# LayerNorm in front of the MLPs: the gain applied with the offset on the turned rows, and to x itself later

## The reference, cut to what matters

```
def layer_norm(x, g, b):
    mu = mean(x); var = mean((x - mu) ** 2)            # over the 2048 channels of a row
    return (x - mu) * rsqrt(var + LN_EPS) * g + b

for i in range(2):
    mix = ssd_mixer(x, ...) if i == 0 else pool_mixer(x, ...)
    x = layer_norm(ALPHA * x + mix, ln_mix_g[i], ln_mix_b[i])                       # the norm in front of the MLP
    x = layer_norm(ALPHA * x + square(relu(x @ w1[i])) @ w2[i], ln_ffn_g[i], ln_ffn_b[i])
```

## Time and profile before

| | |
|---|---|
| median of 3 runs | 2191.07 us (2189.57 to 2195.26) |
| the profiled execution | 2191.99 us, of which its span is 2190.1 us |
| PE busy | 2159.6 us, 99% of the span |
| DVE busy | 1428.4 us, 65% |
| ACT busy | 1119.0 us, 51% |
| POOL busy | 223.3 us, 10% |
| granted PE clock, mean | 0.997 of full speed |

### The profile page before, as it was taken

The page is one execution under the profiler, slowest core; times in us unless marked ns, Lnnn a source line. Parts: engine busy times, 40 slices in busy tenths (PEclk is TensorE's granted clock), DMA queues, the critical chain, the costliest instruction groups (busy, mean ns, idle before and its releaser), DMA issues.

```text
span 2190.1 us, 30795 instructions
## 1 busy us (share of the span) xinstructions
PE 2159.6 (99%) x10626; PEld 1816.4 (83%) x10626; DVE 1428.4 (65%) x1730; ACT 1119.0 (51%) x1565; POOL 223.3 (10%) x172
## 2 busy tenths in 40 slices
PE   9999999999999999999999999989999999999997
PEld 7788888888888788888888888878888888888886
DVE  7787787687777656557565655686565655555656
ACT  5677576675775634444343443456444443443433
POOL 0213233132220100002000000032000000000001
PEclk9999999999999999999999999999999999999999
DMA  7968988589586574545555645445555645555553
GB/s 274 254 202 236 252 230 244 179 235 277 174 249 209 195 252 170 199 172 196 187 193 190 211 172 196 169 154 207 197 197 186 216 167 198 185 190 193 192 192 115
DMA packets 246963, 443.99 MB, mean 203 GB/s; under 512 B 14049, under 2 KB 49041, under 8 KB 245217
## 3 DMA queue, kind: packets, MB, share of 16 engines
q1 hardware_dynamic: 206608, 397.52, 53.5%
q0 software_dynamic: 35664, 28.66, 7.6%
q10 hardware_dynamic: 4608, 16.78, 2.0%
HBM read 440.68 MB, written 2.23 MB: 202 GB/s over the span
## 4 chain that ended last, share of the span: by engine, by line
PE 90%; DVE 4%; ACT 2%; issue 2%; DMA 2%; ACTq 0%; DVEq 0%; SPq 0%
PE acc L375 14%; PE acc L377 14%; PE acc L376 14%; PE acc L638 9%; PE acc L645 5%; PE tb L638 5%; PE sbk L638 5%; PE sbk L377 3%; PE tb L375 3%; PE tb L376 3%; PE sbk L375 3%; PE sbk L376 3%; PE tb L377 3%; PE sbk L645 2%; PE tb L645 2%; DVE wlo L1145 2%
## 5 line engine op out<-in xcount | busy, mean ns | idle before, releaser
L748 ACT CAST whi<-raw 128x1024 fp32r<-128x1024 f32 x746 | 773.8, 1053 | 666.7 <-DMA raw<-in_w 292.3
L1145 DVE TENSOR_TENSOR wlo<-raw,whi 128x1024 fp32r<-128x1024 f32 x746 | 917.0, 1266 | 205.3 <-ACT whi L748 201.5
L375 PE MATMUL acc<-whi,xT 128*128 128x512 f32 x832 | 334.5, 402 | 14.9 <-DVE wlo L1145 9.9
L377 PE MATMUL acc<-wlo,xT 128*128 128x512 f32 x832 | 325.2, 391 | 0.0
L376 PE MATMUL acc<-whi,xT 128*128 128x512 f32 x832 | 324.8, 390 | 0.0
L375 PE MATMUL acc<-whi,hTl 128*128 128x512 f32 x736 | 291.4, 396 | 0.3 <-DVE hTl L1165 0.3
L376 PE MATMUL acc<-whi,hTh 128*128 128x512 f32 x736 | 286.6, 389 | 0.0
L377 PE MATMUL acc<-wlo,hTh 128*128 128x512 f32 x736 | 286.5, 389 | 0.0
L638 PE MATMUL acc<-xT,whi 128*128 128x512 f32 x896 | 224.0, 392 | 0.0
L375 PEld LDWEIGHTS acc<-whi,xT 128*128 128x128 f32 x832 | 156.7, 188 | 53.5 <-issue 10.8
L638 PEld LDWEIGHTS acc<-xT,whi 128*128 128x128 f32 x896 | 162.0, 189 | 29.6
(11 more groups left out here) (210 smaller groups left out, 2667.1 us busy)
## 6 DMA issues: line engine op xcount, KB each, us to landing
raw<-in_w SPq DMA_DIRECT2D x512, 512.0 KB, 4.7
raw<-in_in_proj SPq DMA_DIRECT2D x162, 512.0 KB, 5.6
raw<-in_out_proj SPq DMA_DIRECT2D x64, 512.0 KB, 7.1
spare<-in_masks ACTq DMA_DIRECT2D x16, 512.0 KB, 7.7
spare<-f_scratch POOLq DMA_DIRECT2D x32, 256.0 KB, 15.4
area_d<-in_masks ACTq DMA_DIRECT2D x8, 512.0 KB, 6.3
area_d<-f_scratch POOLq DMA_DIRECT2D x16, 256.0 KB, 7.5
area_c<-in_masks ACTq DMA_DIRECT2D x8, 512.0 KB, 7.0
```

The costliest lines, as they stand in the source:

```text
L375: pe.matmul(dst, lhs[1][:, kt, rows(t)], hi, start=first and i == 0, stop=False)
L377: mm = pe.matmul(dst, lhs[0][:, kt, rows(t)], lo, start=False, stop=end)
L748: act.copy(whi[:, s.slot(RING)], raw[:, r]).then_inc(hi_ready, 1)
L1145: dve.tensor_tensor(wlo[:, slot], raw[:, r], whi[:, slot].bitcast(F32), ALU.subtract).then_inc(lo_ready, 1)
```

## The change

The gain is applied by ACT together with the offset: the four L783 instructions of a quarter get `scale=lng[...]` (one number per partition) beside `bias=lnb[...]`. The turned rows are therefore made from x without its gain, and PE's `x_ready` waits for ACT's norm (`ln_act`) instead of the gain. The seven `gains` instructions and the one `gain_q3` of each norm go; eight `late_gain` instructions on DVE, in the first chunk between the splits s + 12 to s + 19, multiply x itself. POOL's additions of the offset wait for these (`x_gain`). A small load of the gains by rows, `lng`, joins the loads at the start, and the waits for these count one more. The norms behind the MLPs are as before but for the numbers of their semaphores.

```
-LN_BASE = [[0, 10, 20, 30], [0, 11, 21, 32]]
+LN_BASE = [[0, 7, 17, 24], [0, 7, 17, 24]]
...
             def x_ready(i):
                 def ready(t, j):
-                    if t == 0 and j == 3:
-                        pe.wait_ge(t0_gain_q3, i + 1)
-                    else:
-                        pe.wait_ge(ln_vec[t], LN_BASE[t][i] + 8 + j)
+                    pe.wait_ge(ln_act[t], 4 * i + j + 1)
...
                         off = act.activation(offset_x[u % 2][:, k * P:(k + 1) * P], tb[u % 2][:, k * P:(k + 1) * P],
-                                             ACT.Identity, bias=lnb[:, first // 16, kt:kt + 1])
+                                             ACT.Identity, bias=lnb[:, first // 16, kt:kt + 1],
+                                             scale=lng[:, first // 16, kt:kt + 1])
...
-            dve.wait_ge(const_in, 16 * 7)
+            dve.wait_ge(const_in, 16 * 8)
...
+            def late_gain(i, t, j):
+                cs = slice(j * NB, (j + 1) * NB)
+                dve.wait_ge(gb_in, 32 * (i + 1))
+                dve.wait_ge(ln_act[t], 4 * i + j + 1)
+                dve.tensor_tensor(x[:, t, cs], x[:, t, cs], gb[:, 0, cs], ALU.mult).then_inc(x_gain, 1)
...
                 mean_var(i, 0)
                 factors(i, 0)
-                early = len(adds) > 2
-                if early:
-                    adds[0](1)
-                gains(i, 0, (0, 1))
-                if early:
-                    adds[1](1)
-                gains(i, 0, (2,))
-                for add in adds[2 if early else 0:-1]:
+                for add in adds[:-1]:
                     add(1)
...
                 split_lo(s + 5)
-                gains(i, 1, (0, 1))
                 split_lo(s + 6)
                 split_lo(s + 7)
-                gains(i, 1, (2, 3))
                 for j in range(4):
                     lo_x(first, 1, j)
...
-                blocks(s + 8, 2, 4, lambda k: lo_h(u, k) if k < 2 else None)
+                def second(k):
+                    if k < 2:
+                        lo_h(u, k)
+                    for t in range(TT):
+                        late_gain(i, t, k)
+                blocks(s + 8, 2, 4, second)
...
             pool.dma_start(lnb[:], a["ln_b_rows"]).then_inc(const_in, 16)
+            pool.dma_start(lng[:], a["ln_g_rows"]).then_inc(const_in, 16)
...
             def offsets(i, first, s):
-                gain_q3(i)
                 pool.wait_ge(tr_lo, first + 8)
                 for j in range(4):
                     if j > 0:
                         pool.wait_ge(w_used, s + 6 + 4 * j)
                     for t in range(TT):
                         cs = slice(j * NB, (j + 1) * NB)
+                        pool.wait_ge(x_gain, 4 * i + 2 * j + t + 1)
                         pool.tensor_tensor(x[:, t, cs], x[:, t, cs], gb[:, 1, cs], ALU.add).then_inc(x_norm[t], 1)
```

More of the change, by code:

```diff
@@ L136, in build @@
         lnb = sb("lnb", [P, 2, KT])
+        lng = sb("lng", [P, 2, KT])
         warm = sb("warm", [P, 1])
@@ L215, in build @@
         gb_in = sem("gb_in")
+        x_gain = sem("x_gain")
         stored = sem("stored")
@@ L704, in pool_x @@
                 else:
-                    pe.wait_ge(t0_gain_q3, 2)
+                    pe.wait_ge(t0_gain_q3, 1)
                 pe.wait_ge(ln_act[1], 4 + g + 1)
@@ L909, in dt_steps @@
                 if k == 0:
-                    act.wait_ge(const_in, 16 * 7)
+                    act.wait_ge(const_in, 16 * 8)
                     act.wait_ge(dt_vec, 1)
@@ L1741, in _ @@
             pool.wait_ge(ln_vec[0], LN_BASE[0][1] + 10)
-            pool.wait_ge(t0_gain_q3, 2)
+            pool.wait_ge(t0_gain_q3, 1)
             pool.wait_ge(ln_vec[1], LN_BASE[1][1] + 10)
@@ L1757, in _ @@
                 else:
-                    pool.wait_ge(t0_gain_q3, 4)
+                    pool.wait_ge(t0_gain_q3, 2)
                 pool.tensor_tensor(x[:, 0, cs], x[:, 0, cs], gb[:, 1, cs], ALU.add).then_inc(x_norm[0], 1)
@@ L1797 @@
         "ln_b": np.stack([d["ln_mix_b"][0], d["ln_ffn_b"][0], d["ln_mix_b"][1], d["ln_ffn_b"][1]]),
+        "ln_g_rows": np.stack([by_channel(v) for v in d["ln_mix_g"]], axis=1),
         "ln_b_rows": np.stack([by_channel(v) for v in d["ln_mix_b"]], axis=1),
```

## The result

The changed kernel takes 2194.37 us (median of 21 runs, 2192.04 to 2196.88), the kernel before 2191.15 us (21 runs beside them, 2189.51 to 2195.26). The ratio is 1.0013 with a 95% interval of 1.0007 to 1.0018: 1.5 to 3.9 us slower, well within 0.3%, and yet clear of no change. The prediction was 2193.2 us and "no change that can be told".

A forecast was written before the change was run, and what follows sets the result against it. PE was taken as the bound outside the norms, so its waits there count fully. Layer 0 +2.3, layer 1 -0.2 and covered late gains gave +2.1 us on 2191.07: 2193.2 us, range 2188.5 to 2198.0.

The forecast's parts named there:

- Rival A: ACT's second operand is free: layer 0 gains nothing, layer 1 its 1.7 us, 2189.4 us; chance 0.2.
- rival C: The turn waits for something else than the gain; in layer 1 0.9 us less gained, 2194.1 us; chance 0.1.
- The second operand: On ACT, each L783 reads scale beside bias: 0.094 us more each, a group of four from 1.14 to 1.52 us.
- Layer 0's norm: Before layer 0's MLP: PE's first product of tile 0 0.7 us later, 2.3 us later in sum.
- Layer 1's norm: Before layer 1's MLP: 0.92 us earlier at tile 0, 0.76 taken back at tile 1; sum 0.2 us earlier.
- The late gains: First chunk, DVE: six gains of 3.8 us plus 2.2 us of POOL stretching fit 7.2 us idle, 1.2 left.
- rival B: First chunk: DVE stands still for each 3.75 us pair of POOL additions; 4.1 us late per layer, 2201.4 us; chance 0.08.

## Why the prediction was right, and which term was off

- *The time.* Measured 2194.37 us, in the range, and close to the forecast. That alone shows little: the range, 2188.5 to 2198.0, also held rivals A and C. What bears the account out is the stages and the runs. "No change that can be told" went by 0.3%; with 21 runs of each kernel the interval is about 0.06% either way, and a loss of some 3 us shows.
- *What bounds the kernel.* PE without a pause in the loop, so that waits at the norms are neither made up nor given back: the sum of the stages, +3.2 us, is the difference of the medians.
- *The second operand.* Predicted 0.094 us, a group of 1.52 us; measured 0.09 and 1.50. The Trainium skill's timing on "ScalarE: Activation LUTs", section "What ACT_TABLE_LOAD costs", about 93 ns for each pointer operand, agrees with these rows. The free affine of the Trainium skill's section "Step-by-step: what each stage is for" on that page, read as one that takes no time, does not. Rival A falls with the run of the operand alone.
- *Layer 0's norm.* Predicted +0.7 at tile 0's first product and +2.3 up to tile 1's; measured +0.68 and +2.19, by the chain that was written out (split s + 6 came 1.45 us late, as against 1.5). PE's first wait was 0.66 and not about 1 us, since part of the lateness shows as longer transposes (1.33 us at 706.88 instead of 1.03): the run with the operand alone has them at 1.32 too, the one with late gains and no operand at 1.03.
- *Layer 1's norm.* Predicted 0.92 us won at tile 0 and 0.76 lost at tile 1; measured 0.94 and 0.72. PE's wait came down to 0.66, against about 1.0, for the same reason as in layer 0. Without the operand 1.6 us are won, against at most 1.7 predicted: the gains were on the path, and rival C falls.
- *The late gains: the term that was mis-sized.* The step said: six gains of 3.8 us and 2 x 1.1 us of stretching, 6.0 of 7.2 us, covered with 1.2 left. Undisturbed the gains left 3.68 us, against 7.2 - 3.8 = 3.4 reckoned. But the two pairs of additions cost 2.2 us each, not 1.1: four splits grew from 4.63 to 6.82, and four gains from 2.50 to 4.70. 3.68 - 2 x 2.2 is -0.7, and PE was 0.6 us late in each layer. The sign that was named for rival B came: the gap is gone, and PE waits for the low parts of the hidden rows. Where the 1.1 went wrong shows when the runs of equal instructions are taken apart. The kernel before, DVE and POOL, with an undisturbed pair first:

```profile
756.66 2.54 POOL L1726 TENSOR_TENSOR x<-x,area_a 128x512 f32<-128x512 f32 x2 [8.84 <-PE acc L377]
...
765.30 1.52 POOL L1726 TENSOR_TENSOR x<-x,area_a 128x512 f32<-128x512 f32 x1 [6.10 <-PE acc L377]
765.58 2.32 DVE L1145 TENSOR_TENSOR wlo<-raw,whi 128x1024 fp32r<-128x1024 f32 x1
```

and the changed kernel, the first addition of the first pair and three of the four splits:

```profile
751.93 1.62 POOL L1730 TENSOR_TENSOR x<-x,area_a 128x512 f32<-128x512 f32 x1 [2.77 <-DVE x L1369]
752.31 2.33 DVE L1145 TENSOR_TENSOR wlo<-raw,whi 128x1024 fp32r<-128x1024 f32 x1
754.56 2.30 DVE L1145 TENSOR_TENSOR wlo<-raw,whi 128x1024 fp32r<-128x1024 f32 x1
756.79 1.21 DVE L1145 TENSOR_TENSOR wlo<-raw,whi 128x1024 fp32r<-128x1024 f32 x1
```

The 1.1 us is the price of one addition, not of a pair. In the row that it came from the earlier trace rows a single split is stretched, 2.32 instead of 1.21 us; the pair's second addition ended beside a low part of the hidden rows and an `add_x`, which read PSUM and were not stretched (0.68 and 0.69 us). In the changed kernel both additions of a pair met a split or a gain, so each pair stretched two instructions by 1.1 us. The stretched splits ended 1.1 us after the end of the addition beside which they began (765.58 + 2.32 against 765.30 + 1.52, and 752.31 + 2.33 against 751.93 + 1.62), nearly the length of a split: it reads as if DVE waited for that addition. No run tests this by itself.
- *Rival B* is thus half true: its place and mechanism were right, and 2.2 us a pair lies beyond the 1.7 from which it was to decide. Its size, 4.1 us a layer, was not: 0.6 us. It reckoned the stretched 3.75 us of a pair, which hold POOL's own delay, as lost to DVE; a pair alone takes 2.54, and DVE lost 2.2. The Trainium skill's "GPSIMD Engine Reference", section "1. Specifications", says that POOL's SBUF interfaces are shared with DVE, with contention where a DVE instruction has two SBUF inputs; the run with POOL held back agrees (splits 4.62 and gains 2.50 us without POOL beside them, 6.82 and 4.70 with it).
- *The sum.* +2.1 predicted, +3.2 measured; the difference is this one term, 2 x 0.6 us. The other terms were off by about 0.1 us.

## What to carry to other kernels

An operand that looks free because the instruction is there anyway has a price per instruction; multiply it by the instructions that stand before the first wait it can lengthen, and compare that with what the removed work cost at the same wait. When work is moved into another engine's free time, look at what it brings with it: here POOL's additions waited for the moved gains and so came later, closer together and beside DVE's splits, and the two together needed more than the free time that either would have fitted. A price of contention read from one overlap holds for the instructions that met in that row; take the row apart, count them, and count again in the new place.

## What the runs showed of the hardware

A second per-partition operand of ACT costs 0.09 us in each instruction even in back-to-back runs of 128x128 (1.14 to 1.50 us a group of four). Beside POOL's additions, DVE's instructions with two SBUF inputs were stretched (most, not all of them): four gains went from 2.50 to 4.70 us, four splits from 4.63 to 6.82, and to 8.40 where POOL added without a pause; a single split that met an addition went from 1.21 to 2.3 us. DVE's instructions with an input in PSUM were not: L1619, which reads `acc`, took its 0.69 us beside POOL's gains in the run that gave these to POOL, between two L1623 of 1.28 and 1.51. POOL's pair of additions went from 2.54 to 3.85 us.
